# One operand buffer laid out with both parts of a chunk side by side, in two MLP phases of a transformer kernel

## What is computed

```python
def squared_relu_mlp(h, w_up, w_down):
    a = jax.nn.relu(h @ w_up)          # w_up: 1024 x 4096
    return (a * a) @ w_down            # w_down: 4096 x 1024

for i in range(DEPTH):                 # DEPTH = 2
    ...                                # pooling mixer (i = 0) or attention (i = 1)
    h = modulate(rmsnorm(x, norm_mlp[i]), sh2, sc2)
    x = x + g2[:, None, :] * squared_relu_mlp(h, w_up[i], w_down[i])
```

## Time and profile before

| | us |
|---|---|
| median of 3 runs | 1011.12 (1010.39 to 1015.95) |
| profiled execution, its own time | 1013.9 |
| its span | 1012.1 |
| TensorE busy | 977.0 |
| VectorE busy | 788.2 |
| ACT busy | 560.6 |
| GpSimd busy | 105.1 |

### The profile page before, as it was taken

One profiled execution on the slowest core, in us unless ns is written; L12 is line 12 of the kernel. 1 busy time (PEld: TensorE's weight loads), 2 busy tenths in 40 slices (PEclk: granted clock), 3 DMA queues, 4 the chain that ended last, 5 costly groups with the idle time before them and its releaser, 6 DMA issues.

```text
span 1012.1 us, 19319 instructions
## 1 busy us (share of the span) xinstructions
PE 977.0 (97%) x7468; PEld 910.6 (90%) x7468; DVE 788.2 (78%) x1370; ACT 560.6 (55%) x922; POOL 105.1 (10%) x134
## 2 busy tenths in 40 slices
PE   4799999999999999999999999999999999999996
PEld 2479998888989899999888999998889999999996
DVE  4757986999777677667876899999998887777554
ACT  3248675444655567776544666677126564444352
POOL 0000000000000000000000000999910000000000
PEclk8799999999999999999999999999999999999998
DMA  9998798887564865554555455453446555555531
GB/s 378 421 419 336 275 378 300 318 325 280 144 203 115 307 239 177 189 186 167 208 179 213 164 193 170 164 208 127 165 139 221 182 187 189 194 179 190 193 116 42
DMA packets 35880, 222.27 MB, mean 220 GB/s; under 512 B 3883, under 2 KB 9180, under 8 KB 9436
## 3 DMA queue, kind: packets, MB, share of 16 engines
q1 hardware_dynamic: 35804, 221.22, 60.6%
HBM read 220.13 MB, written 1.07 MB: 219 GB/s over the span
## 4 chain that ended last, share of the span: by engine, by line
PE 81%; DVE 8%; DMA 4%; ACT 4%; issue 2%; DVEq 0%; SPq 0%; ACTq 0%
PE bank L656 22%; PE bank L645 17%; PE bank L646 16%; PE bank L650 12%; PE bank L982 5%; PE bank L1035 3%; DMA mod_raw<-w_mod 2%; DVE w_lo L1472 2%; PE s_banks L679 1%; ACT w_hi L1109 1%; DVE s_banks L1879 1%; DVE bank L1854 1%; PE s_banks L1035 1%; DMA raw<-weights 1%; DVE ab L1847 1%
## 5 line engine op out<-in xcount | busy, mean ns | idle before, releaser
L1472 DVE TENSOR_TENSOR w_lo<-raw,w_hi 128x1024 fp32r<-128x1024 f32 x284 | 346.3, 1225 | 32.1 <-ACT w_hi L1109 29.7
L1109 ACT ACTIVATE w_hi<-raw 128x1024 fp32r<-128x1024 f32 x284 | 296.1, 1050 | 93.6 <-PE bank L656 89.9
L645 PE MATMUL bank<-xg_hi,w_hi 128*128 128x258 f32 (+1 forms) x1376 | 340.9, 285 | 0.8 <-ACT w_hi L1109 0.5
L646 PE MATMUL bank<-xg_lo,w_hi 128*128 128x258 f32 (+1 forms) x1376 | 336.5, 281 | 0.0
L645 PEld LDWEIGHTS bank<-xg_hi,w_hi 128*128 128x128 f32 x1376 | 259.7, 189 | 5.8 <-issue 4.7
L646 PEld LDWEIGHTS bank<-xg_lo,w_hi 128*128 128x128 f32 x1376 | 260.1, 189 | 0.2
L656 PE MATMUL bank<-xg_hi,w_lo 128*128 128x258 f32 (+1 forms) x1376 | 198.3, 282 | 0.3 <-DVE w_lo L1472 0.3
L656 PEld LDWEIGHTS bank<-xg_hi,w_lo 128*128 128x128 f32 x1376 | 178.5, 189 | 0.8 <-DVE w_lo L1472 0.5
L650 PE MATMUL bank<-hid,w_hi 128*128 128x512 f32 x512 | 127.7, 391 | 0.0
L650 PEld LDWEIGHTS bank<-hid,w_hi 128*128 128x128 f32 x512 | 91.5, 188 | 15.8
L656 PEld LDWEIGHTS bank<-hid,w_lo 128*128 128x128 f32 x512 | 68.5, 188 | 5.3
(11 more groups left out here) (245 smaller groups left out, 1262.0 us busy)
## 6 DMA issues: line engine op xcount, KB each, us to landing
raw<-weights SPq DMA_DIRECT2D x157, 1024.0 KB, 4.9
mod_raw<-w_mod SPq DMA_DIRECT2D x28, 1024.0 KB, 11.4
mod_raw<-w_dots SPq DMA_DIRECT2D x20, 1024.0 KB, 9.6
toep<-bias_by_distance SPq DMA_DIRECT2D x8, 256.0 KB, 5.4
x<-x_in SPq DMA_DIRECT2D x1, 1024.0 KB, 4.9
toep<-bias_by_distance SPq DMA_DIRECT2D x8, 128.0 KB, 3.9
y_out<-yout SPq DMA_DIRECT2D x4, 256.0 KB, 2.4
c_all<-c_row SPq DMA_DIRECT2D x1, 512.0 KB, 14.8
```

Of the source, the lines that this page charges most:

```text
L645: pe.matmul(dst, hi, r_hi, start=start, stop=False, skip_group_check=True)
L646: pe.matmul(dst, hi, r_lo, start=False, stop=False, skip_group_check=True)
L1109: act.activation(pool_w_hi[:, at, :] if name == "pool" and at < 2 else w_hi[:, at % HL, :], raw[:, slot, (at % 2) * UT * P:(at % 2 + 1) * ...
L1472: ve.tensor_tensor(lo, raw[:, slot, (at % 2) * UT * P:(at % 2 + 1) * UT * P], hi.bitcast(F32), ALU.subtract).then_inc(lo_done, 1)
```

## The change

`hid` becomes one flat buffer that begins on a line and is 64 bytes longer. Layer 0 uses it from its beginning, layer 1 from 64 bytes on. In it each of the 32 chunks has its high part of 256 elements and right behind it its low part, so chunks are 2 KB apart and the operand of an L650 matmul is 512 elements in one run. The users (L839, L843 on TensorE, L1212 on ACT, L1667 on VectorE) address it accordingly. Before, high and low part both began 64 bytes past a line in both layers; after, that is so in layer 1, and in layer 0 both begin on a line. The kernel's other buffers stay where they are. The whole diff:

```diff
--- before.py
+++ after.py
@@ -280,9 +280,10 @@
             pool_hi = sb("pool_hi", [P, DC, SEQ], F32R, part)
             pool_lo = sb("pool_lo", [P, DC, SEQ], F32R, part)
         with ExitStack() as part:
-            half_line("hid", part)
-            hid = sb("hid", [P, 2, FFC, SEQ], F32R, part)
-            hid_hi, hid_lo = hid[:, 0], hid[:, 1]
+            hid = part.enter_context(nc.sbuf_tensor("hid", [P, 2 * FFC * SEQ + HALF], F32R, align_bytes=LINE))
+            hid = {"up0": hid[:, 0:2 * FFC * SEQ], "up1": hid[:, HALF:HALF + 2 * FFC * SEQ]}
+            hid = {name: t.rearrange("p (c h n) -> p c h n", h=2, n=SEQ) for name, t in hid.items()}
+            hid["down0"], hid["down1"] = hid["up0"], hid["up1"]
         with ExitStack() as part:
             qT = sb("qT", [P, 2, SEQ], F32, part)
             kT = sb("kT", [P, 2, SEQ], F32, part)
@@ -836,11 +837,11 @@
                     k = 8 * (j % 4) + s
                     if j < 4:
                         pe.wait_ge(hid_lo_done, base + k + 1)
-                    by_high_once(dst[:, :], (U0[name] + j) % HL, s, hid[:, :, k, :], k == 0)
+                    by_high_once(dst[:, :], (U0[name] + j) % HL, s, hid[name][:, k], k == 0)
                 low_ready(name, i, j)
                 for s in range(UT):
                     k = 8 * (j % 4) + s
-                    mm = by_low(dst[:, 0:SEQ], (U0[name] + j) % HL, s, hid_hi[:, k, :], k == FFC - 1)
+                    mm = by_low(dst[:, 0:SEQ], (U0[name] + j) % HL, s, hid[name][:, k, 0, :], k == FFC - 1)
                 mm.then_inc(pe_units, 1)
                 if name == "down0":
                     mod_work(name, 8 * i + j)
@@ -1209,7 +1210,7 @@
                 base = 0 if name == "up0" else 32
                 act.activation(ub[:, j % 2, :], ab[:, j % 2, 0:SEQ], ACT.Relu, bias=ab[:, j % 2, SEQ:SEQ + 1]).then_inc(relu_done, 1)
                 act.wait_ge(relu_done, 8 * i + (base + j + 1))
-                act.activation(chunk(hid_hi, 8 * i + j), ub[:, j % 2, :], ACT.Square).then_inc(hid_hi_done, 1)
+                act.activation(chunk(hid[name][:, :, 0, :], 8 * i + j), ub[:, j % 2, :], ACT.Square).then_inc(hid_hi_done, 1)
                 act.activation(sb2[:, j % 2, :], ub[:, j % 2, :], ACT.Square).then_inc(sq2_done, 1)
                 if isinstance(i, int):
                     mod_work(name, 8 * i + j)
@@ -1664,7 +1665,7 @@
                 t = 8 * i + j
                 ve.wait_ge(hid_hi_done, 8 * i + (base + j + 1))
                 ve.wait_ge(sq2_done, 8 * i + (base + j + 1))
-                ve.tensor_tensor(chunk(hid_lo, t), sb2[:, j % 2, :], chunk(hid_hi, t).bitcast(F32),
+                ve.tensor_tensor(chunk(hid[name][:, :, 1, :], t), sb2[:, j % 2, :], chunk(hid[name][:, :, 0, :], t).bitcast(F32),
                                  ALU.subtract).then_inc(hid_lo_done, 1)
                 if isinstance(i, int):
                     mod_work(name, t)
```

## The result

The changed kernel took 1014.01 us (median of 10 runs, 1011.87 to 1016.42) against 1012.57 us for the kernel before beside it. The ratio is 1.0024, 95% interval 1.0013 to 1.0035. Two later comparisons gave 1.0016 (1.0003 to 1.0029) and 1.0027 (1.0015 to 1.0039). So it is slower, by some 2 us, and inside the half per cent that was called no change. (The plain medians of the three comparisons differ by 1.4, 1.5 and 2.7 us.) The forecast was 2.7 us faster, and 1014.01 lies above the range, which ended at 1013.0.

A forecast was written before the change was run, and what follows sets the result against it. TensorE was taken to bound down0 and down1. High matmuls -3.3 us and low matmuls +0.6 us gave -2.7 us: 1008.4 us against the median of 1011.12 (1011.2 on the profiled execution's time), range 1003.5 to 1013.0.

The forecast's parts named there:

- What bounds the kernel: In down0 and down1 TensorE alone: busy 88.50 us of the 88.50 us of each stretch, at 2.4 GHz.
- who could be late next: VectorE in down0, 80.42 us busy of 88.50, but it waits 6.5 us on TensorE; nothing subtracted.
- (1): High matmuls (L650), both layers: one run of 512 columns takes 222.5 ns in place of 229, 3.3 us gained.
- best case: High matmuls (L650) at the pace of the full fp32 row L982, 215.9 ns: 6.7 us gained.
- (2): Low matmuls (L656): in layer 0 the step becomes 118 ns, 0.6 us lost; in layer 1 no change.
- The collision rival: Layer 0: weights and moving operand both start on a line and meet at each; net +2.9 us, 1014.0; chance 0.15.
- By columns: Matmuls of both layers: extra cost goes with columns, so contiguity is worth nothing; 1011.1 us; chance 0.25.
- The signs: L650 steps at 222.5 ns, down0 87.3 and down1 86.7 us; wrong if L650 stays within 1 ns of 229.

## Why the prediction was wrong

- *What bounds the kernel, and who could be late next:* right. TensorE is busy for the whole of both phases; VectorE still waits for it 6.0 us in down0. The same start gave the same stage with the parts written at either pitch, so the writes play no part there.
- *(1), the high matmuls: this step failed.* "The 512-column one reads two separate runs, and its extra is about that of two matmuls of one run" was arithmetic, not cause. Measured: 229.0 ns in one run and in two in the kernel, and 228.8 in both by itself. The term of 3.3 us is 0.0 in layer 1, and in layer 0 0.3 us of loss, from the start and not from the runs. The row taken as its best case was misread too, as said above: a record of the earlier trace rows is half an instruction.
- The rows did hold the rival. Its sentence, 0.447 ns a column at 512 and 0.443 at 256, fitted as well; I gave it 0.25 because nothing in the trace spoke for either. The third size is near it: 173.3 ns at 384 columns is 0.451 a column. It is no exact law, for 256 columns also run at 117.8 ns (0.460) at the same place, and 128 take 111.7 ns. What is shown is that the number of runs costs nothing.
- *(2), the low matmuls in layer 0:* the sign and nearly the size were right. I took 118 ns from the pool stage, as the row with equal starts, and it measured 119.1: 0.83 us in place of 0.6.
- *The collision rival* had the right variable: a start at the same place as the weights. Its price, 4.6 us, was four times what it costs (1.12 us), for 512 columns rose by 1.1 ns and not 13. Its support was in part mistaken: it took 113 and 118 ns for the work of addresses, and they are two states at the same addresses. Its condition "slower once a 512-column step in layer 0 is over 231 ns" assumed layer 1's gain, which did not come. I had 0.15 on it; I argued against it with the pool row, though that row's 118 ns *is* the collision.
- *By columns* was right for layer 1 alone. The result is this rival with the small end of the collision.
- The sum: -2.7 us forecast, +1.12 us measured in the two phases, 2.3 us in all. The forecast in microseconds was built on 1011.12 us for the kernel before, which took 1012.57 beside the changed one; on that base its range would have ended at 1014.5. So that 1014.01 lies above it is as much the base's doing; what failed is the direction.
- *The signs:* in layer 0 L650's step moved by 1.1 ns, the wrong way, and in layer 1 not at all. The sign "a stage other than the two changes by more than 1 us" was no test of the change, for w2 differs by 2.3 us between executions of one kernel.
- *The Trainium skill:* "TensorE: Matmul & The Clock Gate" (Back-to-back issue gap), by its formula for an isolated matmul, would have had 215.8 ns for 512 columns; no layout of five starts and two orders came under 228.8 here. That the fp32 rows agreed with it, at 215.9 ns, was by record and not by instruction. By "SBUF — State Buffer" (Door 1: The DMA port swizzle), with lines of 16 bytes, neither contiguity nor 64 bytes should matter. The first held, the second did not: down0 takes 88.27 against 89.39 us.

## What to carry to other kernels

Before a cost is put down to a cause from rows that hold two variables at once (here columns and runs), look for a third size, or give both readings the same chance. With reduced fp32 matmuls at full clock, count the moving operand's start from where the weights start, since it is their difference that matters. Of the differences tried, 64 bytes beyond a multiple of 256 was best; 192 is half a line as well, and cost 0.5 us a phase. A probe whose buffers are of odd sizes varies more than their stated offsets, so work out every address before you compare. When the same instructions on the same addresses show two steady steps, treat the difference as a state that any edit may flip, even in phases that it doesn't touch, and judge an edit by its own stage over several profiles rather than by one total.

## What the hardware showed that was not expected

- A stream of 256-column reduced-fp32 matmuls with chunks 1024 bytes apart, half a line from the weights, settles at one of two exact steps, 113.3 or 117.8 ns, and stays there for a whole phase (w2: 528 matmuls, 2.3 us between the states). In the down phases, between groups of 512 columns, it alternates from unit to unit (113.4 and 118.0 ns). Which one it is depends on place and on what ran ahead.
- The step depends on the moving operand's place relative to the weights, within 256 bytes: 229.0 ns at 64 bytes, 230.1 at 0, 232.8 at 128 and at 192 for 512 columns in the kernel. That the loads of weights are the cause is only inferred from this; no kernel ran without loads.
- At the lower granted clock (0.50) the extra is gone: in the stretch of the earlier trace rows ten steps of 256 columns, from 49.65 us on, take 2.13 us, 213.3 ns each. Full fp32 shows 215.8 ns a record at either start.
